# One broadcast store of the bias table in place of eight, in a two-layer encoder kernel

## The chip, the core and the metric

The kernel runs on one core of one Trainium2 chip. The metric is the device time of one execution in microseconds (us). Before the change the median of three runs is 945.81 us. About 0.2% of that, some 1.9 us, is the least that a measurement of this kernel can tell from no change.

## What is computed

Two layers of an encoder block over 256 tokens of width 1024, in float32. Each layer has a gated feed-forward part, a mixing part with windowed attention beside a spatial gate, and a second feed-forward part:

```python
for l in range(DEPTH):                                   # DEPTH = 2
    x = x + 0.5 * _swiglu(_rmsnorm(x, ffn1_norm[l]), ffn1_w_in[l], ffn1_w_out[l])   # D_FF = 2816
    h = _rmsnorm(x, mix_norm[l])
    p = h @ w_mix_in[l]
    ...
    out_a = _spatial_gating(a_proj, sgu_norm[l], sgu_w[l], sgu_b[l])
    out_b = _windowed_gqa(q, k, v, q_norm[l], k_norm[l], sink[l], rel_bias)
    x = x + jnp.concatenate([out_a, out_b], axis=-1) @ w_mix_out[l]
    x = x + 0.5 * _swiglu(_rmsnorm(x, ffn2_norm[l]), ffn2_w_in[l], ffn2_w_out[l])
```

The part that matters here is the attention's relative-position bias. It depends on (key position minus query position) and on the head alone, is the same in both layers, and is added to the scores:

```python
    rel = np.arange(3 * BLOCK)[None, :] - BLOCK - np.arange(BLOCK)[:, None]
    bias = rel_bias[_t5_bucket(rel)]
    ...
    s = jnp.where(valid, s + bias, NEG_INF)
```

## The kernel before

**The weights are the work.** Every weight matrix is cut into units of 128 x 2048 float32 (1 MB), and position p of a layer names the unit. SyncE loads a unit as two transfers of 512 KB into `raw`, which holds three units (L289 to L295); ScalarE copies it to `w_hi` in a reduced format (L475), VectorE takes the difference into `w_lo` (L662), and TensorE multiplies with three products per tile (L910, L911, L913). `w_hi` and `w_lo` hold six units. SyncE may load position p when `w_lo` of position p - 3 is done; ScalarE may convert p when TensorE has used p - 6. `units_used` counts used units and starts at 6.

**The feed-forward part runs in chunks** of 256 hidden columns, c = 0 to 10. Chunk c needs two input units (positions 3c - 1 and 3c, for c above 0) and one output unit (position 3c + 4). TensorE's order in `chunk(c)` is: both input units for the first 128 tokens, the transposes of h of chunk c - 1 (L965, both token halves), both input units for the second half, then the output unit of chunk c - 1 for both halves. The second transpose waits for `h_done` of the second half, which VectorE counts in `mul` (L668).

**ScalarE and VectorE work in a fixed order**, and an instruction that waits holds everything behind it. In `chunk(c)` ScalarE does the second half's silu of chunk c - 1 (L487), the conversion of the next chunk's first input unit, two evacuations of transposed h (L491), the first half's silu, and the conversions of the next second input unit and of chunk c's output unit. VectorE follows with the same order: `mul`, `w_lo`, `hT_lo` (L674) twice, `mul`, `w_lo`, `w_lo`.

**The bias table** is built by GpSimd in eight partitions of tile `o`, one row of 511 numbers for each head (`brow`). Since each of 128 queries needs the row shifted by one, GpSimd sends it to memory 128 times over (`bias_rows`, 8 x 128 x 511) and reads it back with a row pitch of 510 numbers, so that each partition of `bias` holds its own shift. In before this is one store and one load for each head (L427 and L431, eight times). The store of head hh waits until TensorE has used position 4 + 3 hh of the first layer, and the load waits until the store has landed. `bias` is first read by VectorE in `biased` (L782), in the first layer's mixing part. Behind the loop on GpSimd stand the loads of `ws`, `sgain` and `sinks` (L438 to L440) and the norms of the mixing part.

GpSimd's transfers are on DMA queue q0 of the profile, SyncE's on q1; both run on the same 16 DMA engines.

Of the kernel before, what the change touches and what calls it, by code (L numbers as in the profile page):

```python
# [22 lines left out]
P = 128  # L23
# [12 lines left out]

LAYER_POS = 78
EMPTY = 44
BIAS_AFTER = 4
LAYER_UNITS = LAYER_POS - 1  # L40
FFN_BASE = (0, 45)
POS_KV, POS_Q, POS_V, POS_U, POS_OUT = 33, 34, 36, 38, 40
# [4 lines left out]
def nth(p):  # L47

    return p if p < EMPTY else p - 1
# [39 lines left out]
def encoder(nc, x, ffn1_norm, ffn1_w_in, ffn1_w_out, mix_norm, w_mix_in, sgu_norm, sgu_w, sgu_b,  # L89
            q_norm, k_norm, sink, rel_bias, w_mix_out, ffn2_norm, ffn2_w_in, ffn2_w_out, out):  # L90
    _, S, D = x.shape
    DEPTH = ffn1_w_in.shape[0]
    DFF = ffn1_w_out.shape[1]
# [4 lines left out]
    NH = sink.shape[1]  # L98
# [9 lines left out]
    RELS = 2 * S - 1  # L108
    bias_rows = nc.dram_tensor("bias_rows", (NH, P, RELS), F32, kind="Internal").ap()

    with ExitStack() as ctx:
# [6 lines left out]
        def sem(name):  # L118
            return ctx.enter_context(nc.semaphore(name))
# [51 lines left out]
        brow = o[0:NH, 0:RELS]  # L171
# [16 lines left out]
        bias_stored = sem("bias_stored")  # L188
# [10 lines left out]
        units_used = sem("units_used")  # L199
# [44 lines left out]
        def n_used(L, p, j=0):  # L244
            return L * LAYER_UNITS + j * 6 + (SLOTS + nth(p) + 1)
# [124 lines left out]
        def _(pool):  # L370
# [50 lines left out]
            inverse_rms(0, 0, 1)  # L421


            for hh in range(NH):

                pool.wait_ge(units_used, n_used(0, BIAS_AFTER + 3 * hh))
                pool.dma_start(bias_rows[hh:hh + 1, :, :],  # L427
                               brow[hh:hh + 1, :].unsqueeze(1).to_broadcast([1, P, RELS])).then_inc(bias_stored, 16)
                pool.wait_ge(bias_stored, 16 * (hh + 1))
                src = bass.AP(bias_rows.tensor, hh * P * RELS + (P - 1), [[RELS - 1, P], [1, 3 * P]])  # L430
                pool.dma_start(bias[:, hh, :], src).then_inc(bias_loaded, 16)  # L431

# [780 lines left out]
```

## Time and profile before

| | before |
|---|---|
| median of 3 runs | 945.81 us (945.48 to 946.87) |
| the profiled execution | 945.81 us |
| its span | 944.1 us |
| outside the span | 1.7 us |
| TensorE busy in the span | 923.9 us (98%) |
| VectorE, ScalarE, GpSimd busy | 55%, 46%, 10% |
| DMA | 168.97 MB, mean 179 GB/s |

The profiled execution took just the median, so a sum made against its span goes over to the median without a correction. TensorE is busy nearly throughout; the other engines and the transfers matter where they make it wait. Times of a row are from the start of the span.

### The profile page before, as it was taken

The page shows a single profiled execution, that of the slowest core. Times are in us where ns is not written, and L with a number is a line of the kernel's source. Part 1 is how long each engine was busy: PE and PEld are TensorE (multiplying, and loading weights), DVE is VectorE, ACT ScalarE, POOL GpSimd, SP SyncE. Part 2 cuts the span into 40 slices and gives each one's busy share as a digit, 9 for nine tenths or more (in the row PEclk, how much of TensorE's full clock was granted, in tenths as well). Part 3 has the DMA queues.
Part 4 walks back from the last instruction along what each step waited for, and adds up shares of the span by engine and source line. Part 5 has one row for each costly group of instructions (what it writes and reads, how often), then busy time and mean ns, then how long its engine had stood idle before and what let it go on. Part 6 is the DMA issues. An engine that isn't in the chain of part 4 may idle for free.

```text
span 944.1 us, 13030 instructions
## 1 busy us (share of the span) xinstructions
PE 923.9 (98%) x4434; PEld 768.6 (81%) x4434; DVE 516.0 (55%) x574; ACT 436.9 (46%) x515; POOL 92.4 (10%) x140
## 2 busy tenths in 40 slices
PE   8999999998999999999989999999989999999997
PEld 6888888886888888888878888888868888888886
DVE  5654554566666644455456444464757674554542
ACT  6453443455745434345355343452656463433421
POOL 5000000115400000000010000000434000000000
PEclk9999999999999999999999999999999999999999
DMA  8999999744154674654546745645431566564521
GB/s 268 275 178 263 173 232 225 215 143 168 46 175 153 221 239 147 203 197 155 167 142 234 239 156 195 208 141 201 148 135 36 188 196 205 178 214 161 188 105 44
DMA packets 119320, 168.97 MB, mean 179 GB/s; under 512 B 5805, under 2 KB 98025, under 8 KB 119273
## 3 DMA queue, kind: packets, MB, share of 16 engines
q1 hardware_dynamic: 117408, 163.60, 51.2%
q0 software_dynamic: 1504, 4.73, 7.3%
q8 instruction: 28, 0.46, 0.2%
q14 instruction: 20, 0.16, 0.1%
q10 hardware_dynamic: 360, 0.03, 0.0%
HBM read 165.19 MB, written 3.14 MB: 178 GB/s over the span
## 4 chain that ended last, share of the span: by engine, by line
PE 90%; POOL 4%; issue 2%; DVE 2%; DMA 1%; ACT 0%; POOLq 0%; ACTq 0%; SPq 0%; DVEq 0%
PE U L910 18%; PE U L913 18%; PE U L911 18%; PE D L910 5%; PE D L911 5%; PE D L913 5%; PE C L910 5%; PE C L911 5%; PE C L913 5%; PE TR L965 2%; POOL rstd L402 2%; PE TR L1044 1%; PE D L1075 1%; DMA raw<-in_ffn_w_in_dram 1%; POOL mean L401 1%
## 5 line engine op out<-in xcount | busy, mean ns | idle before, releaser
L662 DVE TENSOR_TENSOR w_lo<-raw,w_hi 128x2048 fp32r<-128x2048 f32 (+1 forms) x154 | 346.4, 2269 | 122.3 <-ACT w_hi L475 122.2
L910 PE MATMUL U<-w_hi,xT_hi 128*128 128x512 f32 (+1 forms) x784 | 309.2, 394 | 3.2 <-issue 2.6
L475 ACT ACTIVATE w_hi<-raw 128x2048 fp32r<-128x2048 f32 (+1 forms) x154 | 287.5, 1894 | 50.4 <-DMA raw<-in_ffn_w_in_dram 29.8
L913 PE MATMUL U<-w_hi,xT_lo 128*128 128x512 f32 (+1 forms) x784 | 304.7, 389 | 0.0
L911 PE MATMUL U<-w_lo,xT_hi 128*128 128x512 f32 (+1 forms) x784 | 303.9, 388 | 0.0
L910 PEld LDWEIGHTS U<-w_hi,xT_hi 128*128 128x128 f32 x784 | 148.6, 190 | 32.0 <-issue 3.0
L913 PEld LDWEIGHTS U<-w_hi,xT_lo 128*128 128x128 f32 x784 | 148.5, 189 | 30.6
L911 PEld LDWEIGHTS U<-w_lo,xT_hi 128*128 128x128 f32 x784 | 148.7, 190 | 28.3
L491 ACT ACTIVATE hT_hi<-TR 128x256 fp32r<-128x256 f32 x88 | 29.4, 382 | 240.1 <-PE TR L965 240.1
L674 DVE TENSOR_TENSOR hT_lo<-TR,hT_hi 128x256 fp32r<-128x256 f32 x88 | 33.6, 419 | 164.8 <-ACT hT_hi L491 164.8
L487 ACT ACTIVATE small<-U,inv 128x256 f32<-128x256 f32 x88 | 41.8, 475 | 115.9 <-PE D L913 79.0
L668 DVE SCALAR_TENSOR_TENSOR small<-U,inv,small 128x256 f32<-128x256 f32 x88 | 42.0, 477 | 64.1 <-ACT small L487 63.8
L910 PE MATMUL D<-w_hi,hT_hi 128*128 128x512 f32 x176 | 69.2, 393 | 0.0
L401 POOL TENSOR_SCALAR mean<-ms 128x1 f32<-128x1 f32 x14 | 5.9, 423 | 645.3 <-ACT sq L503 645.1
L910 PE MATMUL C<-w_hi,hT_hi 128*128 128x512 f32 x176 | 69.0, 392 | 0.0
L911 PE MATMUL D<-w_lo,hT_hi 128*128 128x512 f32 x176 | 68.6, 390 | 0.0
L911 PE MATMUL C<-w_lo,hT_hi 128*128 128x512 f32 x176 | 68.5, 389 | 0.0
L913 PE MATMUL D<-w_hi,hT_lo 128*128 128x512 f32 x176 | 55.6, 390 | 0.0
L913 PE MATMUL C<-w_hi,hT_lo 128*128 128x512 f32 x176 | 54.3, 390 | 0.0
L913 PEld LDWEIGHTS D<-w_hi,hT_lo 128*128 128x128 f32 x176 | 33.1, 188 | 7.0
L913 PEld LDWEIGHTS C<-w_hi,hT_lo 128*128 128x128 f32 x176 | 33.1, 188 | 6.9
L910 PEld LDWEIGHTS C<-w_hi,hT_hi 128*128 128x128 f32 x176 | 33.1, 188 | 6.8
(119 smaller groups left out, 770.5 us busy)
## 6 DMA issues: line engine op xcount, KB each, us to landing
raw<-in_ffn_w_in_dram SPq DMA_DIRECT2D x176, 512.0 KB, 4.8
raw<-in_ffn_w_out_dram SPq DMA_DIRECT2D x88, 512.0 KB, 5.2
raw<-in_w_mix_in_dram SPq DMA_DIRECT2D x28, 512.0 KB, 4.6
raw<-in_w_mix_out_dram SPq DMA_DIRECT2D x16, 512.0 KB, 3.7
bias_rows<-o POOLq DMA_DIRECT2D x8, 255.5 KB, 11.3
bias<-bias_rows POOLq DMA_DIRECT2D x8, 192.0 KB, 6.0
xs<-in_x_dram SPq DMA_DIRECT2D x2, 512.0 KB, 6.5
out_dram<-xs SPq DMA_DIRECT2D x4, 256.0 KB, 2.0
```

Source lines behind the costliest of these rows:

```text
L401: step(pool.tensor_scalar(tmp, src, 1.0 / n, EPS, ALU.mult, ALU.add), L)
L402: return pool.tensor_tensor(dst, tmp, mhalf[:, 0:width], ALU.pow)
L475: act.activation(w_hi[:, p % SLOTS, a:], raw[:, p % RAW, a:], ACT.Copy).then_inc(hi_ready, 1)
L487: act.activation(gate[:, t, :], U[t][:, 0:FC], ACT.Silu, scale=inv[:, t:t + 1]).then_inc(silu_done, 1)
L491: act.activation(hT_hi[:, c % 2, :, t * P:(t + 1) * P], TR[t][:, 0:FC].rearrange("p (k n) -> p k n", k=2), ACT.Copy).then_inc(hT_hi_done, 1)
L662: dve.tensor_tensor(w_lo[:, p % SLOTS, a:], raw[:, p % RAW, a:], w_hi[:, p % SLOTS, a:].bitcast(F32), ALU.subtract).then_inc(lo_ready, 1)
L668: dve.scalar_tensor_tensor(out=h[:, t, :], in0=U[t][:, FC:2 * FC], scalar=inv[:, t:t + 1], in1=gate[:, t, :], op0=ALU.mult, op1=ALU.mult). ...
L674: dve.tensor_tensor(hT_lo[:, c % 2, :, cols], TR[t][:, 0:FC].rearrange("p (k n) -> p k n", k=2), hT_hi[:, c % 2, :, cols].bitcast(F32), AL ...
L910: pe.matmul(out_, x_hi, w_hi[:, slot, c], start=start, stop=False)
L911: pe.matmul(out_, x_hi, w_lo[:, slot, c], start=False, stop=False)
L913: last = pe.matmul(out_, x_lo, w_hi[:, slot, c], start=False, stop=stop)
L965: last = pe.transpose(TR[t][:, kk * P:(kk + 1) * P], h[:, t, kk * P:(kk + 1) * P], ident[:, :])
```

## The change

The wait, the store and the wait for its landing are taken out of the loop over heads. There is one store of all eight rows, 128 times over, which waits for the use of position 6; the load of every head follows after one wait for that store. The position is set by `BIAS_AFTER`, which goes from 4 to 6.

```diff
-BIAS_AFTER = 4
+BIAS_AFTER = 6
...
+            pool.wait_ge(units_used, n_used(0, BIAS_AFTER))
+            pool.dma_start(bias_rows, brow.unsqueeze(1).to_broadcast([NH, P, RELS])).then_inc(bias_stored, 16)
+            pool.wait_ge(bias_stored, 16)
             for hh in range(NH):
 
-                pool.wait_ge(units_used, n_used(0, BIAS_AFTER + 3 * hh))
-                pool.dma_start(bias_rows[hh:hh + 1, :, :],
-                               brow[hh:hh + 1, :].unsqueeze(1).to_broadcast([1, P, RELS])).then_inc(bias_stored, 16)
-                pool.wait_ge(bias_stored, 16 * (hh + 1))
                 src = bass.AP(bias_rows.tensor, hh * P * RELS + (P - 1), [[RELS - 1, P], [1, 3 * P]])
                 pool.dma_start(bias[:, hh, :], src).then_inc(bias_loaded, 16)
```

On GpSimd, between the first two norm steps and the loop over layers, before has the pair of store and load eight times (the first pair is shown; ISA rows are waits and addresses):

```order
L402 TENSOR_TENSOR inv<-mean,mhalf 128x1 [waits pool_step]
L427 DMA bias_rows<-o 128x1x511 [waits units_used]
L431 DMA bias<-bias_rows 128x384 [waits bias_stored]
...
L435 UNCONDITIONAL_BRANCH
L435 ISA
L438 ISA [waits units_used]
L438 DMA ws<-in_sgu_w_dram 128x4x128
```

The same place on GpSimd with the change:

```order
L402 TENSOR_TENSOR inv<-mean,mhalf 128x1 [waits pool_step]
L425 DMA bias_rows<-o 1024x1x511 [waits units_used]
L430 DMA bias<-bias_rows 128x384 [waits bias_stored]
L430 DMA bias<-bias_rows 128x384 x7
L434 UNCONDITIONAL_BRANCH
L434 ISA
L437 ISA [waits units_used]
L437 DMA ws<-in_sgu_w_dram 128x4x128
```

Eight stores of 128 rows became one of 1024 rows, the seven later waits for `units_used` and the seven later waits for `bias_stored` are gone, and seven loads stand one behind the other. The other engines' instructions and their order stay as they were.

## Rows read from the trace of the kernel before

**Rows 1.** The page: busy time by engine, and the chain that ended last.
```profile
PE 923.9 (98%) x4434; PEld 768.6 (81%) x4434; DVE 516.0 (55%) x574; ACT 436.9 (46%) x515; POOL 92.4 (10%) x140
...
PE 90%; POOL 4%; issue 2%; DVE 2%; DMA 1%; ACT 0%; POOLq 0%; ACTq 0%; SPq 0%; DVEq 0%
```

**Rows 2.** Busy time by stretch: stretch, length, engines, TensorE's clock, DMA share, GB/s.
```profile
40.00:60.00 20.00, 20.00 (x92) 16.55 (x91) 8.42 (x7) 6.87 (x8) 1.74 (x3) 1.00 1.03 229
...
160.00:180.00 20.00, 20.00 (x92) 16.58 (x91) 9.87 (x8) 7.02 (x7) 2.68 (x5) 1.00 0.99 237
```

**Rows 3.** Timeline of GpSimd: start, us, what [idle before and its releaser].
```profile
42.15 0.65 POOL L427 DMA_DIRECT2D bias_rows<-o  x1 [26.01 <-PE D L913]
...
58.96 0.53 POOL L427 DMA_DIRECT2D bias_rows<-o  x1 [4.62 <-PE D L913]
70.57 0.56 POOL L431 DMA_DIRECT2D bias<-bias_rows  x1 [11.08 <-DMA bias_rows<-o]
...
197.10 0.19 POOL L401 TENSOR_SCALAR mean<-ms 128x1 f32<-128x1 f32 x1 [23.17 <-ACT sq L503]
```

**Rows 4.** The page's DMA issues: what, count, KB each, us to landing.
```profile
bias_rows<-o POOLq DMA_DIRECT2D x8, 255.5 KB, 11.3
bias<-bias_rows POOLq DMA_DIRECT2D x8, 192.0 KB, 6.0
```

**Rows 5.** DMA queues from 62.2 to 68.4 us: packets, MB, share of 16 engines.
```profile
DMA packets 34, 0.17 MB, mean 27 GB/s; under 512 B 1, under 2 KB 1, under 8 KB 34
...
q0 software_dynamic: 33, 0.17, 91.3%
q1 hardware_dynamic: 1, 0.00, 0.0%
```

**Rows 6.** DMA queues from 54 to 60 us.
```profile
DMA packets 1793, 2.21 MB, mean 369 GB/s; under 512 B 78, under 2 KB 1644, under 8 KB 1793
```

**Rows 7.** Timeline of SyncE's queue.
```profile
43.65 10.23 SPq L295 DMA_DIRECT2D raw<-in_ffn_w_in_dram  x4
55.23 0.95 SPq L295 DMA_DIRECT2D raw<-in_ffn_w_out_dram  x2
63.66 7.05 SPq L295 DMA_DIRECT2D raw<-in_ffn_w_in_dram  x4
```

**Rows 8.** Timeline of TensorE.
```profile
41.23 0.62 PE L913 MATMUL D<-w_hi,hT_lo 128*128 128x512 f32 x2
...
52.83 0.39 PE L913 MATMUL U<-w_hi,xT_lo 128*128 128x512 f32 x1
...
80.73 0.60 PE L965 MATMUL TR<-ident,small 128*128 128x128 f32 x4
...
86.66 0.39 PE L910 MATMUL C<-w_hi,hT_hi 128*128 128x512 f32 x1
```

**Rows 9.** Timeline of ScalarE.
```profile
65.25 3.73 ACT L475 ACTIVATE w_hi<-raw 128x2048 fp32r<-128x2048 f32 x2
70.04 0.48 ACT L487 ACTIVATE small<-U,inv 128x256 f32<-128x256 f32 x1 [1.06 <-PE U L913]
73.35 1.92 ACT L475 ACTIVATE w_hi<-raw 128x2048 fp32r<-128x2048 f32 x1 [2.83 <-DMA raw<-in_ffn_w_in_dram]
```

**Rows 10.** Timeline of VectorE.
```profile
71.63 0.48 DVE L668 SCALAR_TENSOR_TENSOR small<-U,inv,small 128x256 f32<-128x256 f32 x1
75.30 2.29 DVE L662 TENSOR_TENSOR w_lo<-raw,w_hi 128x2048 fp32r<-128x2048 f32 x1 [3.20 <-ACT w_hi L475]
81.56 0.76 DVE L674 TENSOR_TENSOR hT_lo<-TR,hT_hi 128x256 fp32r<-128x256 f32 x2 [3.97 <-ACT hT_hi L491]
```

**Rows 11.** Stretches of 4 us in the first mixing part, columns as in rows 2.
```profile
226.00:230.00 4.00, 1.71 (x18) 1.47 (x19) 0.47 (x1) 0.16 (x1) 3.01 (x2) 1.00 0.56 193
230.00:234.00 4.00, 4.00 (x13) 3.10 (x12) 3.40 (x12) 3.97 (x4) 0.00 (x0) 0.57 0.17 70
```

**Rows 12.** The instructions that touch tile `bias`: durations in ns, first and last start.
```profile
L782 DVE CUSTOM_DVE_ANT_0 sc<-C,bias,sinks x32: 474/480/484, 231.2 to 712.4; 128x256 f32<-128x256 f32 x32
```

## The prediction, made before the changed kernel was run

> **What bounds the kernel now.** I first read the page's busy times and the chain that ended last: TensorE is busy 98% of the span and holds 90% of the chain [rows 1]. So the time changes only where TensorE gains or loses a wait. The busy times by stretch come next. From 40 to 180 us, where all eight stores and loads of the bias run, TensorE is busy 20.00 of 20.00 us in each of seven stretches (the first and the last stand there), at full clock [rows 2]. No wait of TensorE can be taken away there, and what the present stores cost is hidden already.
>
> Then I look at the transfers, which the change touches. GpSimd's timeline shows a store every 16.8 us, the first at 42.15 and so the eighth near 160 us, each followed 11.6 us later by the load that waited for it [rows 3]. A store is small (255.5 KB), yet takes 11.3 us [rows 4]. The DMA queues in the middle of the second store show why that matters: from 62.2 to 68.4 us q0 moved 0.17 MB and filled 91.3% of the engines' time, at 27 GB/s, and q1, the weights, got one packet [rows 5]. With no store in flight the same engines move 369 GB/s [rows 6]. A store therefore stops the weights for its whole length. SyncE had issued a weight unit at 63.66 in that store [rows 7], and ScalarE waited 2.83 us for it, until 73.35 [rows 9]. The store had landed at 58.96 + 11.3 = 70.3, so the unit came 3.1 us after. TensorE did not feel it, since converted units lie ahead of it. Today each freeze of 11 us ends before that lead is used up. The question is how long the single freeze becomes.
>
> **What goes.** Seven waits for `units_used` and seven for `bias_stored` on GpSimd, worth nothing: GpSimd's next work after the loads is at 197.10 us and waits for ScalarE [rows 3], and nobody waits for GpSimd in these stretches. The freezes from 59 to 171 us go too; they cost TensorE nothing [rows 2]. Gain: 0. The loads end earlier than now and VectorE first reads `bias` at 231.2 us [rows 12], so the longer way to the first head's load is covered by over 100 us.
>
> **What moves.** The first store waits for position 6, two units later. TensorE's last product on it starts at 52.83 [rows 8]; for position 4 GpSimd issued at 42.15 [rows 3] what TensorE had ended at 41.23 + 0.62 = 41.85 [rows 8], 0.3 us behind, so the store is issued near 53.5.
>
> **The long store.** It carries 8 x 261,632 B = 2.09 MB. One store's data took 0.262 MB / 27 GB/s = 9.7 us of its 11.3, so 1.6 us are fixed. In each of the eight, all 128 copies are read from one partition. What eight partitions read at once would do no row shows. Bounds: eight partitions each at 27 GB/s give 9.7 us, all eight behind one path of 27 GB/s give 77.5 us; two or four paths give 38.8 or 19.4 us. A full stream of 369 GB/s [rows 6] is 13.7 times 27, over 128 partitions, so if such paths are what limits it, nine partitions share one. If neighbours share in blocks, eight neighbours lie on one or two paths; if the sharing is between far partitions, on up to eight. I take two paths, 38.8 us, which lies nearest the middle of the bounds on the side of neighbours.
>
> The Trainium skill (SBUF — State Buffer, Door 1: The DMA port swizzle) states that partitions 0 to 3 share one port, 4 to 7 another, each at 27.2 GB/s; the trace agrees with the rate, at 27 GB/s, and does not show the mapping. By the page the store takes 38.5 us.
>
> So the store lands near 53.5 + 1.6 + 38.8 = 93.9.
>
> **Who is caught behind it.** Positions 11 and 12 are the four transfers from 43.65 to 53.88 [rows 7]; without a store at 42.15 they are through by then, or nearly. The unit of 55.23 [rows 7], position 13, the output unit of chunk 3, is behind the store. By the second store's example it lands 3.1 us after it, at 97.0. In before ScalarE converted positions 12 and 13 from 65.25 to 68.98 [rows 9]. It now stands at position 13 from 67.2 to 97.0, and behind it on ScalarE is the silu of chunk 3's second half (70.04 now), behind that everything else. VectorE too stands at 13's `w_lo` before the `mul` of 71.63 [rows 10]. TensorE waits for that `mul` at the second transpose of the group of four that starts at 80.73 [rows 8], at 81.0.
>
> The chain after the landing: conversion 97.0, `w_lo` 1.95 later (as 75.30 after 73.35) at 98.95 and 2.29 long, `mul` 0.48, and 0.2 to TensorE: 101.9. TensorE stands from 81.0 to 101.9: **20.9 us**.
>
> **What the stand costs besides.** After 2.3 us of idle time from 226 to 230 us TensorE's granted clock was 0.57 over the next 4 us [rows 11], between its levels of 1.2 and 2.4 GHz: 0.43 x 4 = 1.7 us lost. I add **1.7 us** once; bounds 0 and twice that.
>
> **What comes next.** At 93.9 there are two units (13, 14) and the eight loads of 0.197 MB to move, 3.7 MB, at 369 GB/s some 10 us: position 14 lands by 101 to 104. ScalarE converts it before it evacuates h (chunk(4)'s order). Ready at 102, it is converted by 104, `w_lo` by 106.3, `hT_lo` by 106.7. TensorE has 5.5 us of input products after 101.9 and needs `hT_lo` at 107.6, so I add 0; up to 3 us in the range if 14 lands last. After that no store is left, and the lead grows back. Were a stall to begin earlier, with position 12 caught as well, it would be the same chain from the same landing, within 1 us.
>
> Sum: 945.8 + 20.9 + 1.7 = **968.4 us**.
>
> **The rivals.**
>
> *The weights slip in between (965.6 us).* With 8 x 128 rows a queue can have a turn in the middle of the store. Against it stands one weight packet beside 33 of the store [rows 5]. For it: those stores had only three large packets on each engine, which may all have been taken in before the weights came. Say the queues alternate packet by packet. Packets of the store are some 5.5 KB, so 48 on each of 8 engines. Position 13 needs 16 packets of 4 KB on an engine and is through near 70. Position 14 needs 64 of 1 KB and gets the 32 turns left. The weights' own time lengthens the store by some 4 us, and 14 lands near 100. Conversion, `w_lo` and `hT_lo` take 4.7 us more, and TensorE, which needs them for the output products at 86.66 [rows 8], goes on at 104.8: 18.1 us, and 1.7 for the clock. So even this hardly helps, since each unit needs all engines and ScalarE goes in order. The Trainium skill (DMA: Bandwidth & Descriptors, Queues, rings and completion order) says that an engine takes turns between its queues at each packet; rows 5 speak against it for short stores.
>
> *Not slower (945.8 us).* If eight partitions are read on eight paths, the store lands at 64.8 and position 13 at 67.9, 0.7 us after ScalarE would take it, which the 10 us to TensorE's need hide. The point from which it turns: TensorE waits once the landing is later than 93.9 - 20.9 = 73.0, that is, once the store's data takes over 18 us. Four paths land it at 74.5, for 1.5 us of stall and no clock loss, 947.3. The single large transfer would also have to be as good as full streams are. The Trainium skill (DMA: Bandwidth & Descriptors, Rules for kernel authors) advises at least 1 MiB a transfer and many partitions; the first half of the rule speaks for this change, and its bandwidth would put the store at some 7 us. The stores' 27 GB/s [rows 5] beside 369 [rows 6] says the source is the limit, not the size.
>
> *One path (1007.1 us).* 38.7 us more of the same stall: 945.8 + 59.6 + 1.7.
>
> *Faster (about 943 us).* Fewer freezes would have to shorten a wait of TensorE. It has none between 40 and 180 us [rows 2]; only a shift in the mixing part could do it.
>
> **How the numbers follow.** The long freeze 0.62, alternating packets 0.15, not slower 0.14 (0.10 of it within 0.2%, four paths 0.04), one path 0.06, faster 0.03. Forecast 968.4. The range reaches down to 954, for turns in coarser or finer pieces than I worked out and a faster source, and up to 982 for a source slower than 27 GB/s a path, late position 14 and a second clock loss; it leaves out one path and most of the "not slower" case. Faster by over 0.2%: 0.03, within: 0.10, slower: 0.87.
>
> **What would show it.** Right: one store landing about 40 us after 53.5; q1 nearly silent meanwhile and total flow near 54 GB/s; ScalarE waiting about 30 us for `raw` of `w_out` at L475; TensorE idle some 20 us from 81, then a clock under 1.00; nothing else of the span changed. Alternating: the silence is broken, ScalarE waits at an input unit instead and TensorE stops at L910 into C. Wrong: the store lands before 73 (source paths), or weights flow beside it at over 100 GB/s (no freeze); then the stall is gone. A landing beyond 100 would say one path, or weights that slow the store.

## The result, and the profile after

| | before | after |
|---|---|---|
| median, 4 runs each | 945.64 us | 966.67 us |
| lowest to highest | 943.9 to 946.87 | 965.08 to 968.55 |
| ratio | | 1.0224 (95%: 1.0205 to 1.0243) |
| span of the profiled execution | 944.1 us | 966.3 us |
| TensorE busy | 923.9 us (98%) | 927.9 us (96%) |

The change makes the kernel 2.2% slower. The time lies 1.7 us below the forecast of 968.4 us, inside the range of 954 to 982.

The page's DMA issues of the changed kernel (what, count, KB each, us to landing) answer to [rows 4]: one store of eight times the bytes that takes four times as long, 46.2 us.

```profile
bias_rows<-o POOLq DMA_DIRECT2D x1, 2044.0 KB, 46.2
bias<-bias_rows POOLq DMA_DIRECT2D x8, 192.0 KB, 5.8
```

Who made TensorE wait in the changed kernel (waiting engine and line, releaser, us in total, times, longest):

```profile
PE TR L964 <- DVE small L667: 11.8, 1, 11.8
PE C L909 <- DVE hT_lo L673: 6.7, 1, 6.7
PE TR L1043 <- POOL qs L448: 4.6, 2, 2.3
```

The first two are new, 18.5 us together; the third is in before as well. The forecast had one stall of 20.9 us at the first place. The timeline of ScalarE (start, us, what, idle before and its releaser) shows where both come from:

```profile
64.55 1.93 ACT L474 ACTIVATE w_hi<-raw 128x2048 fp32r<-128x2048 f32 x1
87.49 1.91 ACT L474 ACTIVATE w_hi<-raw 128x2048 fp32r<-128x2048 f32 x1 [21.01 <-DMA raw<-in_ffn_w_out_dram]
89.30 0.46 ACT L486 ACTIVATE small<-U,inv 128x256 f32<-128x256 f32 x1
101.31 1.91 ACT L474 ACTIVATE w_hi<-raw 128x2048 fp32r<-128x2048 f32 x1 [11.54 <-DMA raw<-in_ffn_w_in_dram]
103.12 0.64 ACT L490 ACTIVATE hT_hi<-TR 128x256 fp32r<-128x256 f32 x2
```

Where before converted positions 12 and 13 one behind the other from 65.25 [rows 9], ScalarE now takes 12 at 64.55 and waits 21.01 us for 13. The silu of 70.04 in [rows 9] follows at 89.30. Then it waits 11.54 us for position 14, an input unit, with the evacuation of h behind it. TensorE stops first at the transposes, which need the `mul` after that silu, and then at the output products, which need `hT_lo`.

GpSimd's timeline:

```profile
52.82 1.21 POOL L425 DMA_DIRECT2D bias_rows<-o  x1 [36.36 <-PE U L912]
99.36 4.36 POOL L430 DMA_DIRECT2D bias<-bias_rows  x8 [45.33 <-DMA bias_rows<-o]
```

SyncE's queue, to be set beside [rows 7]:

```profile
54.53 5.30 SPq L295 DMA_DIRECT2D raw<-in_ffn_w_out_dram  x2
62.96 33.31 SPq L295 DMA_DIRECT2D raw<-in_ffn_w_in_dram  x4
```

The store is issued at 52.82 (forecast 53.5) and landed at 99.0 (forecast 93.9). SyncE's issue of the four weight transfers of positions 14 and 15 takes 33.31 us in all, where the same four take 7.05 in [rows 7]; both times include waits for a free buffer. But position 13 was there at 87.49, 11.5 us before the store had landed. So the weights did pass beside the store, if slowly. The DMA queues of the changed kernel from 86 to 95 us, for the most part while TensorE stands, are to be compared with [rows 5]:

```profile
DMA packets 150, 0.54 MB, mean 60 GB/s; under 512 B 4, under 2 KB 73, under 8 KB 150
...
q0 software_dynamic: 75, 0.46, 47.3%
q1 hardware_dynamic: 75, 0.08, 2.5%
```

The store fills half of 16 engines (47.3%), so eight of them, and moves 0.46 MB in 9 us, 51 GB/s. Each of the eight engines takes a store packet every 0.96 us (9 us x 8 / 75). The weights get exactly as many packets, 75, but theirs are of 1 KB here, so they move 0.08 MB in 9 us, 9 GB/s. In this stretch that is the alternation of the prediction's first rival, not a freeze.

How long position 13 took can be read from the DMA queues from 58 to 62 us. Input units have rows of 1 KB and come in packets of that size, output units in packets of 4 KB. In this stretch every packet under 2 KB is also under 512 B, so no packet of an input unit moved: position 12 had arrived by 58, and 13 was on its way.

```profile
DMA packets 149, 0.47 MB, mean 116 GB/s; under 512 B 50, under 2 KB 50, under 8 KB 149
```

From 58 to 87.49 us are 31 turns of 0.96 us, and an engine has 16 packets of position 13 to move. So about half of the turns passed without a weight packet.

TensorE's clock (stretch, length, busy times, granted clock, DMA share, GB/s) shows the rest of the loss:

```profile
84.00:88.00 4.00, 0.00 (x0) 0.00 (x0) 0.00 (x0) 0.51 (x1) 0.00 (x0) 0.59 0.52 69
92.00:96.00 4.00, 3.83 (x12) 3.15 (x13) 0.12 (x1) 0.00 (x0) 0.00 (x0) 0.63 0.49 59
100.00:104.00 4.00, 0.00 (x0) 0.00 (x0) 0.75 (x1) 2.69 (x4) 4.00 (x8) 0.72 0.99 352
104.00:108.00 4.00, 1.99 (x5) 1.61 (x6) 4.00 (x5) 2.04 (x2) 1.54 (x3) 0.50 1.02 387
108.00:112.00 4.00, 4.00 (x11) 3.13 (x10) 1.46 (x2) 1.91 (x1) 0.00 (x0) 0.50 1.04 337
```

During each of the two stalls the clock falls to the lower of its two levels, 1.2 GHz, and stays there for some us after work begins again. Counting busy time alone: 3.83 x 0.37 + 1.99 x 0.5 + 4.00 x 0.5 = 4.4 us, for two stalls. TensorE's busy time as a whole grew by 4.0 us (927.9 against 923.9). The spans differ by 22.2 us; 18.5 of it are stalls, which leaves 3.7 for the clock and all small differences elsewhere. So the clock cost some 4 us.

### The profile page after: what moved, and what is told of

Its sections match the earlier page's. It is cut to its first block, busy times and chain, and to the rows that moved or that the text cites. A ratio compares the mean times of both kernels' runs of the same rounds, so it can differ in the third digit from the quotient of the medians.

```text
span 966.3 us, 13023 instructions
## 1 busy us (share of the span) xinstructions
PE 927.9 (96%) x4434; PEld 770.6 (80%) x4434; DVE 515.9 (53%) x574; ACT 437.1 (45%) x515; POOL 89.2 (9%) x133
## 4 chain that ended last, share of the span: by engine, by line
PE 85%; DMA 5%; POOL 4%; issue 3%; DVE 2%; ACT 1%; SPq 0%; ACTq 0%; POOLq 0%; DVEq 0%
PE U L909 17%; PE U L912 17%; PE U L910 16%; PE D L909 5%; PE D L910 5%; PE D L912 5%; PE C L909 5%; PE C L910 5%; PE C L912 5%; DMA raw<-in_ffn_w_in_dram 5%; PE TR L964 2%; POOL rstd L402 2%; PE TR L1043 1%; PE D L1074 1%; POOL mean L401 1%
## 5 line engine op out<-in xcount | busy, mean ns | idle before, releaser
L910 PEld LDWEIGHTS C<-w_lo,hT_hi 128*128 128x128 f32 x176 | 33.6, 191 | 6.9
## 6 DMA issues: line engine op xcount, KB each, us to landing
bias_rows<-o POOLq DMA_DIRECT2D x1, 2044.0 KB, 46.2
```

The costliest lines, as they stand in the source:

```text
L910: pe.matmul(out_, x_hi, w_lo[:, slot, c], start=False, stop=False)
```

## The experiments

The open question after the result was the cause of the long store: the source partitions, the size or the number of engines, or the place in the program. Theory A has two parts. The eight source rows lie behind two paths of 27 GB/s, and on the engines of the store the weights share turns packet by packet. The rivals are B, the later place; C, one large transfer on eight engines is slow whatever it reads; D, the weights wait for the store's length.

### The place alone

```diff
 # kernel before
-BIAS_AFTER = 4
+BIAS_AFTER = 6
```

> The kernel before, with only BIAS_AFTER at 6: eight stores, each two units later. Theory A (the source: eight rows lie behind two paths of 27 GB/s, and while the store runs each engine it uses gives the weights one packet for one of its own): each store still takes about 11 us, TensorE gains no wait, 945.6 us, same as before. Theory B (the later place in the program makes the stall): about 966 us with TensorE waiting near 81 us.

Measured: 944.7 us against 944.49, ratio 1.0003 (0.9993 to 1.0013). TensorE has no new wait, and each store is issued 11.6 us later. The other half, the merged store at the old place:

```diff
 # changed kernel
-BIAS_AFTER = 6
+BIAS_AFTER = 4
```

> The changed kernel, with BIAS_AFTER back at 4: the merged store is issued near 42 us. Theory A: store of 46 us, same starvation of the weights, TensorE stalled 18 to 27 us (the lead may be shorter this early), 964 to 973 us. Theory B (the place makes the stall): no stall, 945.6 us.

Measured: 970.64 us in one run. The store in the page's DMA issues of that kernel:

```profile
bias_rows<-o POOLq DMA_DIRECT2D x1, 2044.0 KB, 45.6
```

The first row of who made its TensorE wait:

```profile
PE C L909 <- DVE hT_lo L673: 24.4, 1, 24.4
```

At position 4 the store takes the same 46 us and the stall is 24.4 us, in one piece. So the place costs nothing by itself, and of the two edits the merged store is the one that costs. B falls. The place does shape the loss, though. ScalarE's timeline in this kernel shows what was caught first:

```profile
88.86 1.91 ACT L474 ACTIVATE w_hi<-raw 128x2048 fp32r<-128x2048 f32 x1 [30.47 <-DMA raw<-in_ffn_w_in_dram]
```

Here it is an input unit, position 11, with 64 packets of 1 KB for each engine. It came 2 us after the store had landed (41.29 + 45.6 = 86.9), and so the stall lasted until then.

### Where the rows lie

```diff
 # changed kernel; small_rows is a tensor of 8 x 511 in memory
+pool.dma_start(small_rows, brow).then_inc(bias_stored, 16)
+pool.wait_ge(bias_stored, 16)
+pool.dma_start(o[0:32:4, 0:RELS], small_rows).then_inc(bias_stored, 16)
+pool.wait_ge(bias_stored, 32)
 pool.wait_ge(units_used, n_used(0, BIAS_AFTER))
-pool.dma_start(bias_rows, brow.unsqueeze(1).to_broadcast([NH, P, RELS])).then_inc(bias_stored, 16)
-pool.wait_ge(bias_stored, 16)
+pool.dma_start(bias_rows, o[0:32:4, 0:RELS].unsqueeze(1).to_broadcast([NH, P, RELS])).then_inc(bias_stored, 16)
+pool.wait_ge(bias_stored, 48)
```

> The changed kernel, with its eight rows first moved to partitions 0, 4, 8 ... 28 by a small transfer through memory at 16 us, then the one store of 2044 KB from there at position 6. Theory A: each row is read on a path of its own, the eight engines run at up to 27 GB/s each, data in 10 us and with the weights' turns some 15, landing 15 to 20 us after issue, no wait of TensorE, 945.6 us. Theory C (one transfer of 1024 rows from GpSimd's queue on eight engines is slow wherever its rows lie): landing after about 46 us, 966 us.

Measured: 944.03 us, ratio 0.9994 (0.9982 to 1.0007): the whole loss is gone with the same transfer from other partitions. The store in the page's DMA issues of this kernel:

```profile
bias_rows<-o POOLq DMA_DIRECT2D x1, 2044.0 KB, 27.7
```

Its DMA queues from 62 to 74 us:

```profile
DMA packets 1135, 2.24 MB, mean 187 GB/s; under 512 B 40, under 2 KB 882, under 8 KB 1135
...
q1 hardware_dynamic: 965, 1.20, 44.0%
q0 software_dynamic: 170, 1.04, 36.2%
```

The same 12 us in the changed kernel:

```profile
q0 software_dynamic: 96, 0.59, 45.1%
q1 hardware_dynamic: 646, 0.88, 25.3%
```

With the rows apart the store moves 87 GB/s (1.04 MB in 12 us), above the 54 of two paths, where it moved 49; and the weights move at 100 GB/s beside it, where they had 73. (The 9 GB/s above are those of 86 to 95 us.) A store packet now occupies its engine for 0.41 us (36.2% x 16 x 12 us / 170), against 0.91 in the changed kernel (47.3% x 16 x 9 us / 75). C falls. The landing after 27.7 us misses the 15 to 20 that were expected. The engines also had weights to move, which took 44.0% of their time against the store's 36.2%; that this is the whole reason was argued and not tried. The run also shows that the landing time is not what decides: the prediction's turning point, a landing by 73.0, would give a stall at the transposes for this store, which landed at 52.95 + 27.7 = 80.7 and gave none. All that is new among TensorE's waits is 0.9 us at the output products.

The opposite edit puts the eight rows on one path, if the Trainium skill's map holds (SBUF — State Buffer, Door 1: The DMA port swizzle: partitions 32 to 35 share the port of 0 to 3):

```diff
 # changed kernel
+pool.dma_start(small_rows, brow).then_inc(bias_stored, 16)
+pool.wait_ge(bias_stored, 16)
+pool.dma_start(o[32:36, 0:RELS], small_rows[4:8, :]).then_inc(bias_stored, 16)
+pool.wait_ge(bias_stored, 32)
...
+for q in range(2):
+    pool.dma_start(bias_rows[4 * q:4 * q + 4, :, :],
+                   o[32 * q:32 * q + 4, 0:RELS].unsqueeze(1).to_broadcast([4, P, RELS])).then_inc(bias_stored, 16)
+pool.wait_ge(bias_stored, 64)
```

> The changed kernel, with rows 4 to 7 moved to partitions 32 to 35 and the store cut in two (rows 0 to 3, rows 4 to 7) issued one behind the other without a wait between. Theory A, with the Trainium skill's map (SBUF, Door 1: partitions 0 to 3 and 32 to 35 share a port): total 27 GB/s, last landing 80 to 90 us after issue, packets twice as long (1.8 us against 0.9), TensorE stalled some 55 us, about 1003 us. If the path is not shared: 54 GB/s, 46 us, about 966 us.

Measured: 1007.1 us in one run, with two stalls of 29.6 and 28.0 us. GpSimd's timeline in this kernel:

```profile
54.00 2.25 POOL L431 DMA_DIRECT2D bias_rows<-o  x2 [31.93 <-PE U L919]
141.44 4.38 POOL L437 DMA_DIRECT2D bias<-bias_rows  x8 [85.19 <-DMA bias_rows<-o]
```

Its DMA queues from 104 to 128 us:

```profile
q0 software_dynamic: 107, 0.66, 48.9%
q1 hardware_dynamic: 106, 0.10, 1.2%
```

Both stores together move 0.66 MB in 24 us, 27 GB/s, half the changed kernel's rate, and the last lands 87 us after the first issue. A turn is now 24 x 8 / 107 = 1.79 us, nearly twice 0.96. The map holds for these four partitions, and the weights again get one packet for one in this stretch (106 and 107). The edit also makes two stores of one; that this alone does not halve the rate is seen in the last experiment, where two stores from partitions 0 to 7 move 50 GB/s together.

### More engines, more partitions

Two kernels copy each row to several partitions by the same small transfer, so that the source is `o[0:16]` (64 copies each) or `o[:]` (8 copies each):

```diff
 # e7_sixteen_rows
+pool.dma_start(o[0:16, 0:RELS], small_rows.unsqueeze(1).to_broadcast([NH, 2, RELS])).then_inc(bias_stored, 16)
...
+pool.dma_start(bias_rows.rearrange("h (r c) n -> (h r) c n", r=2),
+               o[0:16, 0:RELS].unsqueeze(1).to_broadcast([16, 64, RELS])).then_inc(bias_stored, 16)
 # e5_all_partitions
+pool.dma_start(o[:, 0:RELS], small_rows.unsqueeze(1).to_broadcast([NH, 16, RELS])).then_inc(bias_stored, 16)
...
+pool.dma_start(bias_rows.rearrange("h (r c) n -> (h r) c n", r=16),
+               o[:, 0:RELS].unsqueeze(1).to_broadcast([P, 8, RELS])).then_inc(bias_stored, 16)
```

> The changed kernel, with each row first copied to two neighbouring partitions, so that the one store reads partitions 0 to 15, 64 times each, with 16 engines on four paths. Theory A: 108 GB/s, packets as long as in the changed kernel (0.9 us, four engines on a path), 22 of them on each engine, landing about 25 us after issue, stall of TensorE 0 to 3 us, 946 to 949 us. If the number of paths did not matter but that of engines did: half the changed kernel's rate per engine is gone either way, landing still about 25 us, so this run sets the point from which the stall begins, not the cause.

> The changed kernel, with each row first copied to 16 partitions (a small transfer through memory at 16 us), so that the one store reads all 128 partitions, 8 times each. Theory A (paths of 27 GB/s and turns by packet): 16 engines on 16 paths, the store's data near full rate, landing within 15 us of its issue, no wait of TensorE, 945.6 us, same as before. Theory C (one transfer of 1024 rows is slow wherever its rows lie): 966 us.

Measured: 949.78 us for sixteen rows, ratio 1.0048 (1.0031 to 1.0064), one new stall of 4.6 us, both somewhat above the 946 to 949 us and 0 to 3 us expected; 945.19 us for all partitions, ratio 1.0007 (0.9994 to 1.0021), no new stall. The rows of ScalarE's timeline at which it gets position 13 follow. With the rows on eight paths:

```profile
71.75 1.92 ACT L479 ACTIVATE w_hi<-raw 128x2048 fp32r<-128x2048 f32 x1 [5.52 <-DMA raw<-in_ffn_w_out_dram]
```

With all partitions:

```profile
75.20 1.92 ACT L480 ACTIVATE w_hi<-raw 128x2048 fp32r<-128x2048 f32 x1 [8.65 <-DMA raw<-in_ffn_w_out_dram]
```

With sixteen rows:

```profile
80.50 1.91 ACT L480 ACTIVATE w_hi<-raw 128x2048 fp32r<-128x2048 f32 x1 [13.84 <-DMA raw<-in_ffn_w_out_dram]
```

The prediction's chain puts 4.9 us between that start and TensorE, which needs it near 81 (80.4 in the changed kernel), so the stall at the transposes should begin past about 76. It does: 71.75 and 75.20 give none there, 80.50 gives 4.6 us. This is the point from which it decides, and it is a point of unit 13's arrival, not of the store's. The stores of eight paths (27.7 us) and sixteen rows (26.9 us) take nearly the same time to land, with a stall there in the second alone. All partitions took 22.0 us, more than the 15 expected; here too the weights shared the engines.

### In two halves

```diff
 # changed kernel
-pool.wait_ge(units_used, n_used(0, BIAS_AFTER))
-pool.dma_start(bias_rows, brow.unsqueeze(1).to_broadcast([NH, P, RELS])).then_inc(bias_stored, 16)
-pool.wait_ge(bias_stored, 16)
+for q in range(2):
+    pool.wait_ge(units_used, n_used(0, BIAS_AFTER + 9 * q))
+    pool.dma_start(bias_rows[:, 64 * q:64 * q + 64, :],
+                   brow.unsqueeze(1).to_broadcast([NH, 64, RELS])).then_inc(bias_stored, 16)
+pool.wait_ge(bias_stored, 32)
```

> The changed kernel, with its store in two halves of 64 copies, the first at position 6 and the second at position 15, three chunks (50 us) later. Theory A with a lead that covers the first 18 us or so of each: each half lands some 25 us after issue, stall 0 to 3 us for each, 946 to 951 us. A theory in which the stall is simply proportional to the store's time, without a lead: two stalls of 9 us, about 966 us.

Measured: 953.66 us, ratio 1.0098 (1.0078 to 1.0118), two new stalls of 3.1 and 1.8 us, the halves landing after 24.3 us on average. The median lies 2.7 us above the top of what A expected. The span of the profiled execution is 950.8 us, 6.7 above before; 4.9 of it are the stalls, and the other 1.8, the clock after them and whatever else, was left out of the expectation. That execution took 952.48 us; the median lies another 1.2 us above it, for which there is no profile. The stall is much less than proportional (4.9 us for the same bytes against 18.5), so there is a lead that hides the first part of each store, and a store of half the length is just too long for it.

### All eight small stores at once

```diff
 # changed kernel
-pool.dma_start(bias_rows, brow.unsqueeze(1).to_broadcast([NH, P, RELS])).then_inc(bias_stored, 16)
-pool.wait_ge(bias_stored, 16)
+for hh in range(NH):
+    pool.dma_start(bias_rows[hh:hh + 1, :, :],
+                   brow[hh:hh + 1, :].unsqueeze(1).to_broadcast([1, P, RELS])).then_inc(bias_stored, 16)
+pool.wait_ge(bias_stored, 16 * NH)
```

> The changed kernel, with the one store replaced by the eight single-row stores of before, all issued together at position 6, and the loads after one wait for all. Every one reads a single partition with all 16 engines, so 27 GB/s in all and 78 us or more of store by every theory, about 1000 to 1010 us. It tells turns from a freeze: with turns packet by packet, q1 gets about as many packets as q0 (24 on each engine, some 380 in 78 us); with a freeze for the length of the store q1 gets next to none between 58 and 130 us.

Measured: 997.72 us in one run, a little below the 1000 to 1010 expected, with stalls of 43.6 and 4.6 us. The loads start 76.7 us after the first issue, as GpSimd's timeline shows, so the stores run at 27 GB/s throughout:

```profile
52.38 4.25 POOL L426 DMA_DIRECT2D bias_rows<-o  x8 [36.36 <-PE U L914]
129.12 4.48 POOL L432 DMA_DIRECT2D bias<-bias_rows  x8 [72.50 <-DMA bias_rows<-o]
```

The DMA queues of this kernel from 60 to 125 us:

```profile
q0 software_dynamic: 456, 1.85, 92.0%
q1 hardware_dynamic: 622, 1.38, 5.4%
```

In 65 us the weights got 622 packets. So even the single-row stores, which showed one weight packet against 33 in [rows 5], let the weights through once they are many; a freeze for the store's length is refuted here too. But the sharing is uneven: from 62 to 74 us q1 had 16 packets against 87 of q0, from 78 to 86 us 67 against 53. It also settles what the merging alone did. Eight small stores cost nothing because of the 5 us between them, in which the weights catch up, and 76.7 us without a gap cost more than the merged store's 46.2.

### Wider weight rows, and a shorter turn

If a unit needs fewer packets, it needs fewer turns. The feed-forward input weights are read here as rows of 4 KB of other columns; so neither kernel multiplies with the reference's columns, while sizes and order stay.

```diff
 # load_in, in the changed kernel (e10) and in the kernel before (e11, the control)
-d = dst.rearrange("p (k g n) -> p k g n", k=4, g=2)
 for g in range(2):
-    cols = bass.ds(j * (2 * FC) + (g * DFF + c * FC), FC)
-    yield d[:, :, g, :], w_in[f][bass.ds(L, 1), :, 4 * u:4 * u + 4, cols][0]
+    cols = bass.ds(j * (2 * FC) + (g * 1024 + c * FC), D)
+    yield dst[:, g * D:(g + 1) * D], w_in[f][bass.ds(L, 1), :, 4 * u, cols][0]
```

> The changed kernel, with the feed-forward input weights read as rows of 4 KB in place of 1 KB (other columns of the matrix than the reference asks for, so the products are not the reference's; sizes and order stay). Theory A (turns packet by packet on the eight engines of the store, 0.94 us each): an input unit needs 16 turns in place of 64. Unit 13 lands near 76, unit 14 near 91, the stall goes from 18.5 us to some 9 to 12, the run to 11 to 14 us above its control. Theory D (the weights wait for the store's length, whatever their packets): stall of 18 to 21 us as in the changed kernel.

> The control: the kernel before with the same rows of 4 KB for the feed-forward input weights (again not the reference's columns). TensorE bound, so the same time as before within 0.3%, 944 to 947 us, by both theories.

Measured: 964.88 us, ratio 1.0202 (1.0177 to 1.0227), against 945.24 us, ratio 1.0003 (0.9989 to 1.0017), for the control. The loss is 19.6 us, almost as large as with narrow rows: the expectation of A failed. The timeline of ScalarE in the kernel with wide rows says where:

```profile
66.29 1.93 ACT L473 ACTIVATE w_hi<-raw 128x2048 fp32r<-128x2048 f32 x1
90.25 1.91 ACT L473 ACTIVATE w_hi<-raw 128x2048 fp32r<-128x2048 f32 x1 [22.03 <-DMA raw<-in_ffn_w_out_dram]
...
102.82 1.91 ACT L473 ACTIVATE w_hi<-raw 128x2048 fp32r<-128x2048 f32 x1 [10.30 <-DMA raw<-in_ffn_w_in_dram]
```

The expectation had unit 13 land 11 us earlier. But 13 is an output unit, whose rows are 4 KB in both kernels, and unit 12, the input unit before it, had come through in time in both. SyncE had issued the whole of 13 by 61.3 us here, and it came at 90.25: 30 turns of 0.96 us for 16 packets on an engine, so that again nearly half of the turns passed without a weight packet. The DMA queues of this kernel show both kinds of stretch. From 64 to 67 us:

```profile
q0 software_dynamic: 24, 0.15, 47.0%
q1 hardware_dynamic: 15, 0.05, 10.2%
```

From 85 to 94 us:

```profile
q0 software_dynamic: 75, 0.46, 43.3%
q1 hardware_dynamic: 73, 0.27, 7.2%
```

Unit 14 needed 16 turns here, which after 90.25 come to 105.6; it was there at 102.82, as the store landed (54.55 + 48.4 = 103.0). The edit could have helped only later units.

The stalls are 12.8 and 5.4 us, 18.2 together: that is what D expected (18 to 21), and not what A did (9 to 12). The counts above still speak against D, since the weights had packets in every stretch looked at. But A's steady turn by turn is not what happened either.

This run also bears on another explanation, that SyncE can't issue and the weights are late for that. The issues of positions 14 and 15, from the instructions that touch `raw` (count, durations in ns, first and last start), in the changed kernel and in the one with wide rows:

```profile
L295 SPq DMA_DIRECT2D raw<-in_ffn_w_in_dram x4: 1347/3747/23402, 63.0 to 72.9; - x4
L295 SPq DMA_DIRECT2D raw<-in_ffn_w_in_dram x4: 1388/3906/4166, 64.7 to 74.8; - x4
```

The longest fell from 23.4 to 4.2 us, and the loss stayed. Unit 13 had left SyncE by 59.8 and 61.3 us, some 28 us before it arrived. So a held issue is not what made it late.

The last experiment shortens the store's rows:

```diff
 # changed kernel
-pool.dma_start(bias_rows, brow.unsqueeze(1).to_broadcast([NH, P, RELS])).then_inc(bias_stored, 16)
-pool.wait_ge(bias_stored, 16)
+for a, z in ((0, 256), (256, RELS)):
+    pool.dma_start(bias_rows[:, :, a:z],
+                   brow[:, a:z].unsqueeze(1).to_broadcast([NH, P, z - a])).then_inc(bias_stored, 16)
+pool.wait_ge(bias_stored, 32)
```

> The changed kernel, with its store cut into columns 0 to 255 and 256 to 510, issued one behind the other, so that a row is 1 KB and a packet some 4 KB in place of 6. Theory A: the turn shortens to some 0.6 us, the store's data still takes about 39 us. Unit 13 lands near 78 in place of 87, so the first stall (at the transposes) shrinks from 11.8 to 0 to 4 us, but unit 14 needs 64 turns and lands only once the store is over, near 104, so the second stall (at the output products) grows; the sum stays near 20 us and the time near 967 us. Theory D: first stall as in the changed kernel or longer.

Measured: 971.24 us in one run, with one stall of 23.9 us at the transposes: the opposite of A's expectation, and again what D expected (the first stall as in the changed kernel or longer). Unit 13 came at 99.45, between the landings of the two parts at 95.6 and 100.9. Its DMA queues from 73 to 79 us:

```profile
q0 software_dynamic: 66, 0.30, 92.5%
q1 hardware_dynamic: 1, 0.00, 0.0%
```

And from 79 to 94 us:

```profile
q0 software_dynamic: 210, 0.75, 88.3%
q1 hardware_dynamic: 198, 0.58, 9.7%
```

The two stores ran on all 16 engines (92.5%), still at 50 GB/s together, so that each engine's turn was longer, 6 x 16 / 66 = 1.45 us, and no engine was left free. So the edit changed two things at once, the packets and the number of engines, and is no clean test of the turn's length. The weights got one packet in the first 6 us and nearly one for one in the next 15. "One weight packet for one store packet" is thus what some stretches show, not a rate to count on: there are others with next to none (1 against 66 here, 1 against 33 in [rows 5]), and unit 13 used only about half of its turns in the changed kernel. What withholds the weights in them was not settled.

## Why the prediction was right, point by point

**What bounds the kernel**: right. Nothing between 40 and 180 us could be gained. The seven short freezes that went brought nothing: with one store from well-placed rows the kernel was as fast as before (944.03 us, ratio 0.9994).

**The store's length**: the value of two paths, 38.8 us, was right for the source (51 GB/s measured, and 27 with one path). Its landing came at 99.0 in place of 93.9. It took 46.2 us in place of 40.4. An engine has 43 store packets (128 rows, three to a packet of 6.1 KB; the rival's 5.5 KB and 48 packets were somewhat off), and 43 turns of 0.96 us are 41.3, so 2.5 us came with the rate: of a turn 0.91 us are the store's packet and 0.05 the weights' (2.5% x 16 x 9 us / 75). The other 3.3 us lie outside the data, where 1.6 had been read off a store of 128 rows and 4.9 were needed.

**Who is caught behind it**: right in the unit (13) and in the order of ScalarE and VectorE behind it, wrong in the reason for its arrival. The step "by the second store's example it lands 3.1 us after it" failed. The prediction took the one weight packet beside 33 [rows 5] as a freeze for the whole store; in the long one the weights got turns, about every second one, and 13 came at 87.49, not at 97.0. The long freeze had been given a chance of 0.62, the alternating packets 0.15. Of the signs named for the two, those of both appeared: ScalarE waited for the output unit (21.01 us, not 30), and then at an input unit, with TensorE stopped at the output products. The chain from there to TensorE took from 87.49 to the transposes' start at 92.17, 4.7 us, against 4.9 forecast. The first stall was 11.8 us in place of 20.9.

**What comes next**: the term "I add 0" failed by 6.7 us. The forecast let position 14 land by 101 to 104, and it did, at 101.3. But it started from a TensorE that went on only at 101.9 and had 5.5 us of input products before it. As the first stall was 9 us shorter, TensorE came to the output products at 99.4 and met the unit there.

**The clock**: 1.7 us forecast for one stall, some 4 measured for two (3.7 as what is left of the spans).

**The sum**: 20.9 + 0 + 1.7 = 22.6 forecast, 11.8 + 6.7 + 3.7 = 22.2 measured. That the total is so near is in part luck, since two errors cancel: with its freeze and the landing as it was, 99.0, the prediction would have come to 13 at 102.1, a stall of 26.0 us and 973.5 us. In part it is not luck. By the forecast and as measured, unit 14 arrives only as the store ends, and the output products start within a narrow span of time: at 107.6 by the prediction, at 106.01 as measured. The rival "the weights slip in between" had this end, 965.6 us, and is the nearer description: its stall at the output products is there and its packets alternate. It had 13 through near 70 and so missed the first stall, since it counted on a weight packet in each turn. Neither of the two had the mechanism whole.

**The rival "not slower"** had the right mechanism with the wrong key: its case was brought about by moving the rows (944.03 us), yet the point from which it turns is unit 13's arrival at about 76 us, not a landing at 73.0. **One path** was priced at 1007.1 us and measured, in one run of the experiment, at 1007.1. That the digits agree is luck: one stall of 59.6 us was priced, and two of 29.6 and 28.0 came, with more lost to the clock.

## What to carry to other kernels

Before merging small transfers, ask which partitions the merged one reads, and what its gaps were good for: a store that repeats a few neighbouring partitions ran here at 27 GB/s for each group of four, in a small store (27 from one partition) as in a large one (51 from eight), and the traffic that shares its engines is slowed for as long as it lasts. The same 2 MB cost nothing when its rows were spread over partitions 0, 4 ... 28 or over all 128, at the price of two small transfers. Compare the longest stretch in which the prefetch gets less than it needs with the lead that the buffers hold, here some 23 us (the store issued at 52.8, unit 13 needed by 76); and look for the in-order engine at which the first late unit holds up work that has nothing to do with it.

## What the runs showed of the hardware

- Four neighbouring partitions share one path of 27 GB/s for reads by DMA, and partitions 32 to 35 share that of 0 to 3: eight rows on 0 to 7 moved at 51 GB/s, on 0 to 3 and 32 to 35 at 27, on 0, 4 ... 28 at 87 with weights beside them at 100. Sixteen rows on 0 to 15 moved 98 GB/s (1.17 MB from 62 to 74 us), near four such paths.
- A transfer whose source has eight partitions used eight of the 16 engines (47.3% of their time); with sixteen or 128 source partitions more than eight were in use (81.9% from 62 to 74 us, 66.2% from 57 to 70). Two such transfers, issued one behind the other, used all 16 (92.5%).
- GpSimd's store and SyncE's loads share the engines. Stretches of one packet for one were seen in four kernels (75 and 75, 107 and 106, 75 and 73, 210 and 198). As the store's packets were of 6 KB from a slow source and the loads' of 1 KB, the loads fell to 9 GB/s in the first of these. At other times the loads got far less than their turn (1 against 66), and once somewhat more (67 against 53).
- SyncE's issues were held up during the store: one took 23.4 us with loads of 1 KB rows, and at most 4.2 with rows of 4 KB, without a gain in time.
- After each of TensorE's two stalls, 11.8 and 6.7 us, the granted clock was at 1.2 GHz when work began again. The two cost some 4 us; the one in the forecast was put at 1.7.
